# The fourth projection tile between two groups of index heads, and ScalarE's split of the sixth tile between their relus

## The reference

```python
h = x @ w_in
q_a, c_kv, q_idx, k_idx, w_idx, q_b, k_b, v_b, f_in = _split(h, EVEN_WIDTHS)
q_idx = q_idx.reshape(bsz, seq, H_IDX, D_IDX) * (D_IDX ** -0.5)      # 8 index heads of 64
w_idx = w_idx * (H_IDX ** -0.5)
log_f = jax.nn.log_sigmoid(f_in + b_f);  cum_f = jnp.cumsum(log_f, axis=1)
...
idx = jnp.einsum('bthd,bsd->bths', qi, k_idx)                        # per index head
score = jnp.einsum('bth,bths->bts', wi, jax.nn.relu(idx))            # weighted sum over the 8 heads
score = jnp.where(causal[None], score, -jnp.inf)
_, sel = lax.top_k(score, k_sel)                                     # 64 keys per query
...                                                                  # two attentions of 8 heads each follow
return jnp.concatenate([o_a, o_b], axis=-1) @ w_o
```

## Time and profile before

| what | value |
|---|---|
| time, median of 3 runs | 1373.32 us (1372.79 to 1374.16) |
| time of the profiled execution | 1374.36 us |
| its span, first to last instruction | 1373.1 us |
| mean granted TensorE clock | 0.997 |
| PE busy | 1344.3 us, 98% |
| DVE busy | 1019.8 us, 74% |
| ACT busy | 783.6 us, 57% |
| POOL busy | 178.1 us, 13% |
| PE's share of the chain that ended last | 87% |

### The profile page before, as it was taken

How to read it: one execution, slowest core, us unless ns; L and a number is a source line. 1 busy time by engine, 2 the same in 40 slices (tenths; PEclk the granted TensorE clock), 3 DMA queues, 4 the chain that set the end, 5 groups by cost and what they waited for, 6 DMA issues and landing times.

```text
span 1373.1 us, 20770 instructions
## 1 busy us (share of the span) xinstructions
PE 1344.3 (98%) x8207; PEld 1162.4 (85%) x8207; DVE 1019.8 (74%) x1684; ACT 783.6 (57%) x1260; POOL 178.1 (13%) x155
## 2 busy tenths in 40 slices
PE   7999999999999999999989999999999999999998
PEld 7887888888898888887977788888689998888887
DVE  5865488777887787778777577767567998787666
ACT  5644366565442566663667466555456875665553
POOL 4770300000100000000015200000212224000000
PEclk9999999999999999999999999999999999999999
DMA  8623165645563456542514165655344445355551
GB/s 314 228 78 123 70 231 212 239 184 184 192 246 123 184 194 255 195 184 95 213 62 156 59 230 201 224 201 187 144 163 163 146 154 185 132 205 200 189 196 74
DMA packets 37215, 240.85 MB, mean 175 GB/s; under 512 B 4096, under 2 KB 6528, under 8 KB 9728
## 3 DMA queue, kind: packets, MB, share of 16 engines
q1 hardware_dynamic: 37120, 239.54, 47.7%
HBM read 236.89 MB, written 2.64 MB: 174 GB/s over the span
## 4 chain that ended last, share of the span: by engine, by line
PE 87%; DVE 7%; ACT 2%; issue 2%; DMA 1%; POOL 1%; SPq 0%; DVEq 0%; ACTq 0%; POOLq 0%
PE ps L385 23%; PE ps L437 16%; PE ps L390 12%; PE ps L448 8%; PE ps L365 5%; PE ps L366 5%; PE ps L372 5%; PE ps L609 2%; PE ps L604 2%; DVE wlo L318 1%; PE ps L977 1%; PE ps L580 1%; PE ps L1932 1%; ACT whi L295 1%; PE ps L2247 1%
## 5 line engine op out<-in xcount | busy, mean ns | idle before, releaser
L318 DVE TENSOR_TENSOR wlo<-raw,whi 128x2048 fp32r<-128x2048 f32 (+1 forms) x178 | 399.7, 2251 | 111.5 <-ACT whi L295 109.4
L295 ACT ACTIVATE whi<-raw 128x2048 fp32r<-128x2048 f32 x203 | 385.7, 1904 | 85.2 <-PE ps L448 39.2
L385 PE MATMUL ps<-XS,whi 128*128 128x512 f32 x1392 | 331.7, 390 | 0.0
L385 PEld LDWEIGHTS ps<-XS,whi 128*128 128x128 f32 x1392 | 257.8, 188 | 52.3 <-issue 0.8
L437 PE MATMUL ps<-whi,MS 128*128 128x512 f32 x960 | 233.6, 391 | 0.0
L437 PEld LDWEIGHTS ps<-whi,MS 128*128 128x128 f32 x960 | 177.5, 188 | 35.9 <-issue 0.4
L303 POOL TENSOR_TENSOR wlo<-raw,whi 128x512 fp32r<-128x512 f32 x114 | 154.6, 1389 | 285.2 <-ACT whi L295 197.2
L390 PEld LDWEIGHTS ps<-XS,wlo 128*128 128x128 f32 x1392 | 178.5, 191 | 6.8
L390 PE MATMUL ps<-XS,wlo 128*128 128x256 f32 x1392 | 180.6, 283 | 0.0
L365 PE MATMUL ps<-XS,whi 128*128 128x256 f32 x672 | 168.3, 290 | 0.0
L366 PE MATMUL ps<-XS,whi 128*128 128x256 f32 x672 | 164.4, 284 | 0.0
(11 more groups left out here) (327 smaller groups left out, 1536.3 us busy)
## 6 DMA issues: line engine op xcount, KB each, us to landing
raw<-in_up SPq DMA_DIRECT2D x88, 1024.0 KB, 4.8
raw<-in_down SPq DMA_DIRECT2D x44, 1024.0 KB, 5.0
raw<-in_hg_t SPq DMA_DIRECT2D x16, 1024.0 KB, 4.8
raw<-in_od_t SPq DMA_DIRECT2D x8, 1024.0 KB, 5.4
raw<-in_ev_a SPq DMA_DIRECT2D x6, 1024.0 KB, 9.5
raw<-in_wa_o SPq DMA_DIRECT2D x6, 1024.0 KB, 4.8
raw<-in_hg_o SPq DMA_DIRECT2D x6, 1024.0 KB, 4.7
raw<-in_ev_o SPq DMA_DIRECT2D x4, 1024.0 KB, 5.7
```

The lines of the kernel that those rows point to most:

```text
L295: ac.activation(parts_of(m)[0][:, 0:w], raw[m % NRAW][:, 0:w], ACT.Copy).then_inc(w_hi)
L318: ve.tensor_tensor(lo[:, c], r[:, c], hi[:, c].bitcast(F32), ALU.subtract).then_inc(w_lo_v)
L385: pe.matmul(banks[i][:, 0:512], hi[:, c], XS[:, k, 0:512], start=(k == 0), stop=False)
```

## The change

On PE the fourth projection tile moves from behind the eighth index head to between the fourth and the fifth. On ACT the split of the sixth tile moves from behind the eighth relu to between the fourth and the fifth. No instruction is added, taken away or changed; POOL, DVE and SP keep their order.

```diff
             for h in range(0, 8, 2):
-
+                if h == 4:
+                    project(ea + 3, bank[4])
                 pe.wait_ge(e_ac.sem, 3 + h // 4)
                 if h >= 4:
                     pe.wait_ge(e_re.sem, h - 2)
@@
                         if tt == 1:
                             ins.then_inc(e_ix.up())
-            project(ea + 3, bank[4])
             project(ea + 4, bank[5])
             project(ea + 5, bank[6])
@@
             for h in range(8):
+                if h == 4:
+                    act_weights(ea + 5)
                 ac.wait_ge(e_ix.sem, h + 1)
                 if h >= 2:
                     ac.wait_ge(e_sc.sem, 2 * h - 2)
                 ac.activation(RR[h % 2], bank[h % 4][:, 0:384], ACT.Relu).then_inc(e_re.up())
-            act_weights(ea + 5)
```

## The result

The changed kernel takes 1380.38 us, the median of 20 executions (1372.54 to 1387.01), against 1372.82 for the kernel before (20 executions, 1370.81 to 1374.16). The ratio is 1.0047, with a 95% interval of 1.0036 to 1.0058: slower, and beyond the range's end of 1378.0. The executions of before lie within 3.4 us; those of the changed kernel are spread over 14.5, six up to 1375.8 and fourteen from 1377.4 on, without a clear gap between them. The profiled one is a long one: 1382.79 us, span 1381.5, mean clock 0.995.

The account below looks back on a forecast made before the run. PE, with 87% of the chain of waits, was taken as the bound. A gain of 3.9 us against 5.5 of new waits on POOL gave +1.6 us: 1374.9 us on the median of 1373.32, range 1371.0 to 1378.0.

Parts of the forecast that it names:

- Is DVE late as well?: DVE's first maximum, 30.6 us behind its wide group's start, comes at 89.0 at the latest; no extra time counted.
- I count nothing: At PE's second score, the 1.3 us after DVE's first maximum ends are left to ACT's exponentials; no cost added.
- What PE gains at once: PE's first stage: tile ea + 4 starts at 43.9 instead of 47.81, 3.9 us from waits, slow clock and broken flow.
- What ACT and DVE lose: Index heads: two L1342 wait for POOL, 1.0 to 1.1 us apiece; score complete at 48.8, 5.9 us late.
- what hangs on the score: Log-sigmoid, split of ea + 6 and POOL's low parts come later; PE's new waits 3.1 to 5.5 us, upper end taken.
- the forecast's number: Sum over the first stage: -3.9 + 5.5 = +1.6 us.
- Clearly slower: Rival, PE's new waits on POOL: clock falls behind the second, nothing absorbs it; +3.2, 1376.5 us; chance 0.28.

Follow-up runs that it names:

- e3: Changed kernel with PE's move alone, ACT's split left behind the eighth relu: 1381.23 us, ratio 1.0055 to the kernel before.
- e5: PE's move alone, with the mask's first instruction writing to PSUM: 1373.30 us, ratio 1.0004 to the kernel before.
- ACT's half: Changed kernel with ACT's move alone, PE's tile left behind all heads: 1380.48 us, ratio 1.0053 to the kernel before.
- the long run: Kernel before plus six spare POOL pieces ahead of tile ec: 1373.13 to 1375.99 us (four executions) and 1382.80 to 1384.71 (six), ratio 1.0051.
- POOL holding: Changed kernel, with POOL stopping before the last tile of its run until DVE's mask is made: 1376.00 us, ratio 1.0017.

## Why the prediction was wrong

**The step that failed is "Is DVE late as well?", with its "I count nothing".** It let the first maximum come 30.6 us behind DVE's wide group, "at 89.0 at the latest", as before. The group came even earlier than forecast (57.02 for 58.4), but the 30.6 us contain a mask that met only the end of POOL's run. The forecast had itself made POOL late by 4.5 us and more, and did not ask whether POOL would still have a break where DVE reaches the mask. It had none until 93.05; the maximum came at 93.84. PE then waited 4.48 us at a score that had not waited before (its lag grew from 1.62 to 6.26), and under the slow clock it lost another 3.9 (from 6.26 to 10.17): 8.5 together, of which 1.6 came back near 703 us. This execution stands 7.1 above the 1375.69 of the kernel whose mask could not be kept out. In the second profile of before the mask's first instruction was kept out too, for two pieces (2.75 us), and it cost nothing: the run ended at 81.63. That early end is what the change took away. Even with turns the maximum came at 90.22, 1.2 later than "at the latest", which the 1.3 us that the forecast had left to ACT just covered.

**What PE gains at once.** Counted from the first head, the low part of tile ea + 4 began 12.89 us later (49.73), and 16.60 in the profile before (51.65): 3.7 gained, near the 3.9 forecast. But the first profile of before is one of the slow ones here: over the six profiles of before's stage the distance is 14.04, 14.05, 14.05, 15.18, 16.60 and 16.68, so the gain is 1.2 where heads 6 and 7 wait only 0.6 us, and 2.2 on average.

**What ACT and DVE lose, and what hangs on the score.** One L1343 waited for POOL, not two (3.88 for eight, 1.1 more than 8 x 0.345). The score was complete at 49.64 for 48.8, with heads 1.79 late; the split of ea + 6 ended at 56.08 for 55.5. PE's waits were 1.40, 1.03 and 0.25, 2.7 in sum, at the same three places as forecast and below its 3.1 to 5.5. The 5.5 that the forecast took is twice that. With what the matmuls around the waits lose, PE is 3.5 later: from the low part of ea + 4 to the first score it needs 33.64 us, 30.10 before. This mechanism was right, and its size too large.

**The sum of the first stage.** First scores at 83.37, 83.97, 83.89 and 84.06 with both halves moved, against 81.75, 80.56, 82.45, 81.54, 81.10 and 81.14 in the six profiles of before's stage: 83.8 and 81.4 on average, +2.4, and +2.0 in the time of the kernel with the mask in PSUM (1375.69 against 1373.73 beside it). Counted from the first head, which the change does not touch, it is 46.8 and 45.2: +1.6. That this is the forecast's number is luck: the gain was overstated by 1.7 us (3.9 for 2.2), what the waits cost by as much (5.5 for 3.8, the mean of the four), and the errors cancel. What it weighed against each other are the two halves: with PE's alone (profiles e3, e5) PE needs 32.13 and 32.17 us from the low part of ea + 4 to the first score, with both halves 33.64 to 34.68, so the early split adds 1.5 us or more; in time, with the mask in PSUM, it is +2.0 against +0.3.

**The rivals.** "Clearly slower" had the right sign and the right price list, a wait and a slow clock that nothing takes up, but put it behind the waits on POOL at 62 to 70 us, where the clock stayed 1.00. It came 25 us later, with a wait for another engine.

**The rule that was cited.** The Trainium skill (page "SBUF — State Buffer", section "SBUF: two separate sides") makes the shared ports a lock for the whole instruction, held by whoever starts first. That an instruction with two SBUF inputs waits, L1343 bears out (1.1 us). L1387 has one SBUF input; the section "Who interferes with whom" of the same page also counts tensor_scalar among the operations that can contend with GpSimd for this pair, if its operands allow a mode that uses both ports. No run here shows the mode, but with its output in SBUF it lasted 1.47 us or more in all nine profiles, while with its output in PSUM it took 0.56. If it had to wait only for the GpSimd instruction that holds the pair, that would be one piece; it stood behind three (ACT's half), seven (the changed kernel) and twelve (the long run).

## What to carry to other kernels

Where VectorE and GpSimd share a stage, look for the breaks in GpSimd's queue: a change that makes GpSimd late can close the break that a critical VectorE instruction lives on, and that instruction may then wait for the whole run and not for one piece. A result kept in PSUM takes an instruction out of that contest, but the next one takes its place as long as the run lasts. And read a gain that is made of waits in a second profile: a wait that hangs on when an engine arrives can be gone in the next execution.

## What the runs showed of the hardware

- A VectorE instruction can be passed over by GpSimd instructions that are queued without a break: 12 pieces, 15.06 us, for one that takes 0.56 with its output in PSUM. In another execution of the same program it waited for one piece (1.49 us). Of the nine profiles with this output in SBUF, four have it wait for one piece and five for two to twelve; in one of the five (ACT's half) it got in after three while POOL's run went on. What decides this stays open. In the changed kernel L1387 began 0.05 us after a piece began in the execution where it was kept out (84.37) and in the one where it took its turn (84.96), so the moment of arrival does not tell them apart; L1022 was kept out though it came in the middle of a piece.
- The length of PE's wait does not by itself decide what the clock does. With a wait of 2.67 us at 703 us it fell to 0.50 in the profile before, with 2.66 us at the same place it stayed at 1.00 in the profile after; with 1.65 and 1.71 us at the heads it fell, with 1.74 (the long run with the mask in PSUM) and with 2.43 us (POOL holding, at 63.32) it did not.
- The first 35 us differ from one execution to the next by up to 2.4 us (heads at 35.05 to 37.50), in part by when the matmul L858 can start (18.73 to 20.13), in part by how long the clock is 0.50 between 17.8 and 26 us: from L858 to the heads it takes 16.1 and 16.3 us in the two profiles in which the clock stays 1.00, 16.4 to 17.3 with 3.4 us of 0.50, and 17.5 or 17.6 with 6.8. The stage takes some of it back: of before's profiles the one with the earliest heads has one of the latest first scores.
